# Where the top-k selection steps stand in the dilated branch's merge

## What is computed

```
proj = h @ w_in                                  # h = rmsnorm(x)
ya = forgetting_attention(qa, ka, va, log_f) * silu(za)     # branch A
yb = dsa_attention(qb, k, v, q_idx, kidx, widx) * silu(zb)  # branch B: top-256 keys per query by an indexer score
yc = dilated_attention(qc, kc, vc) * silu(zc)               # branch C
merged = sigmoid(ga)*(ya @ w_a) + sigmoid(gb)*(yb @ w_b) + sigmoid(gc)*(yc @ w_c)
out = rmsnorm(x + merged @ w_o)
```

## Time and profile before

| | us |
|---|---|
| median of 3 runs | 1481.98 |
| profiled execution, own time | 1478.63 |
| its span | 1476.6 |
| PE busy | 1416.3 (96%) |
| DVE busy | 715.2 (48%) |
| ACT busy | 686.4 (46%) |
| POOL busy | 72.0 (5%) |
| PE busy in the merge of branch C, 457 to 679 | 215.98 of 222 |

### The profile page before, as it was taken

How to read it: one execution, slowest core, us unless ns; L and a number is a source line. 1 busy time by engine, 2 the same in 40 slices (tenths; PEclk the granted TensorE clock), 3 DMA queues, 4 the chain that set the end, 5 groups by cost and what they waited for, 6 DMA issues and landing times.

```text
span 1476.6 us, 21005 instructions
## 1 busy us (share of the span) xinstructions
PE 1416.3 (96%) x7910; PEld 1121.4 (76%) x7910; DVE 715.2 (48%) x1618; ACT 686.4 (46%) x1510; POOL 72.0 (5%) x138
## 2 busy tenths in 40 slices
PE   5998899999999999999999989999999999999998
PEld 4976677777767777887777777777777778888786
DVE  4548655555656965463433444533343345222633
ACT  5457776667764531113555565454443533212312
POOL 3033100000000000000000000000000000000000
PEclk8999999999999999999999999999999999999999
DMA  6046111111111112222101001312223222232422
GB/s 207 22 116 156 50 37 29 36 30 36 37 36 29 44 43 79 78 72 72 30 22 29 23 15 52 106 37 72 72 72 101 58 86 51 64 81 70 167 89 100
DMA packets 107875, 96.26 MB, mean 65 GB/s; under 512 B 8320, under 2 KB 93696, under 8 KB 107520
## 3 DMA queue, kind: packets, MB, share of 16 engines
q1 hardware_dynamic: 96528, 58.21, 14.7%
q0 software_dynamic: 11248, 36.71, 7.9%
HBM read 72.62 MB, written 18.09 MB: 61 GB/s over the span
## 4 chain that ended last, share of the span: by engine, by line
PE 80%; DVE 5%; ACT 3%; issue 2%; DMA 0%; ACTq 0%; DVEq 0%; POOL 0%; POOLq 0%
PE bank L793 19%; PE bank L795 19%; PE bank L794 19%; PE bank L987 6%; PE bank L968 6%; PE slot L959 4%; PE slot L944 2%; DVE idle_out L1406 1%; PE slot L793 1%; PE slot L794 1%; PE slot L795 1%; ACT pta L1259 1%; ACT ptb L1259 1%; PE bank L913 1%; DVE tm L1663 0%
## 5 line engine op out<-in xcount | busy, mean ns | idle before, releaser
L793 PE MATMUL bank<-hs,w_hl 128*128 128x512 f32 x1088 | 436.4, 401 | 6.4 <-DVE tm L1663 5.5
L795 PE MATMUL bank<-hs,w_hl 128*128 128x512 f32 x1088 | 426.2, 392 | 0.0
L794 PE MATMUL bank<-hs,w_hl 128*128 128x512 f32 x1088 | 425.2, 391 | 0.0
L1379 DVE TENSOR_TENSOR w_hl<-w_raw,w_hl 128x512 fp32r<-128x512 f32 (+1 forms) x168 | 113.7, 678 | 342.7 <-ACT w_hl L1078 341.8
L793 PEld LDWEIGHTS bank<-hs,w_hl 128*128 128x128 f32 x1088 | 205.3, 189 | 48.6 <-issue 9.1
L795 PEld LDWEIGHTS bank<-hs,w_hl 128*128 128x128 f32 x1088 | 205.0, 188 | 44.6
L794 PEld LDWEIGHTS bank<-hs,w_hl 128*128 128x128 f32 x1088 | 205.6, 189 | 39.9
L1078 ACT ACTIVATE w_hl<-w_raw 128x512 fp32r<-128x512 f32 (+1 forms) x168 | 103.9, 621 | 171.0 <-PE bank L795 162.0
L1406 DVE TENSOR_SCALAR_CACHE_REDUCE idle_out<-score,state 128x768 uint8<-128x768 f32 (+3 forms) x140 | 115.4, 824 | 4.8
L1277 ACT ACTIVATE idle_out<-score,state 128x896 bf16<-128x896 f32 x64 | 70.3, 1098 | 17.1 <-DVE state L1402 16.0
L1576 DVE CUSTOM_DVE_ANT_0 slot<-slot,score 128x128 f32<-128x128 f32 (+7 forms) x64 | 47.3, 781 | 45.9 <-PE slot L959 45.9
(11 more groups left out here) (311 smaller groups left out, 2204.3 us busy)
## 6 DMA issues: line engine op xcount, KB each, us to landing
w_raw<-in_w_in_dram SPq DMA_DIRECT2D x136, 256.0 KB, 2.8
merged_scratch<-ms POOLq DMA_DIRECT2D x16, 512.0 KB, 3.6
ms<-merged_scratch POOLq DMA_DIRECT2D x16, 512.0 KB, 4.1
xn<-in_x_dram SPq DMA_DIRECT2D x8, 512.0 KB, 5.8
iq_st<-iq_hl POOLq DMA_DIRECT2D x32, 128.0 KB, 3.3
qb<-qb_scratch POOLq DMA_DIRECT2D x8, 512.0 KB, 5.0
w_raw<-in_w_o_dram SPq DMA_DIRECT2D x16, 256.0 KB, 3.7
qb_scratch<-bq_high POOLq DMA_DIRECT2D x4, 512.0 KB, 3.1
```

The lines of the kernel that those rows point to most:

```text
L793: pe.matmul(out_, wh, mh, start=start, stop=False)
L794: pe.matmul(out_, wh, ml, start=False, stop=False)
L795: return pe.matmul(out_, wl, mh, start=False, stop=stop)
L1379: v.tensor_tensor(lo, src, hi.bitcast(F32), ALU.subtract).then_inc(w_low, 1)
```

## The change

The counter that placed a step after every third piece goes. After each piece the code looks at the last block step in the list. A selection step is placed only if that piece was of half 0 and the tile is a gate tile `gc` (either base), or has base 0 and is an output tile `wc` or the gate-path tile `zc` 2 or 4. The loop that emptied the queue after the merge is replaced by an assertion that it is empty.

```
-    pieces = 0
     while fill:
         pump(1)
-        pieces += 1
-        if pieces % 3 == 0:
+        a = next(a for kind, a in reversed(plan) if kind == "block")
+        b = blocks[a["n"]]
+        if a["th"] == 0 and (b["kind"] == "gc" or b["base"] == 0 and (b["kind"] == "wc" or b["c"] in (2, 4))):
             pick()
     flush()
-    while picking:
-        pick()
+    assert not picking
```

## The result

The changed kernel takes 1472.45 us (median of 6 runs, 1470.39 to 1473.6), the kernel before in the same rounds 1480.78 (median of 6, 1478.51 to 1484.78). The ratio is 0.9939 with a 95% interval of 0.9927 to 0.995, so 8.3 us by the medians and 7.4 to 10.8 us by the interval. The forecast was 1475.2 us, with a range of 1471.8 to 1478.6, and a saving of 6.8.

The account below looks back on a forecast made before the run. PE was taken to set the end, idling only at bank waits in branch C's merge. Terms -7.0 + 0.2 = -6.8 us took the median 1481.98 to 1475.2 us, range 1471.8 to 1478.6.

Parts of the forecast that it names:

- four gaps: PE idles in the merge of branch C at zc2, after zc3, at zc5 and wc0; removing these saves 7.0 us.
- The dense bit steps: Bit steps 26 to 31, close together in gc0, gc1, wc0 and gc2; cost taken as 0.2 us.
- 13.45 worked out: In gc0, ACT's tanh of half 1 ends 13.45 us after the tile's first matmul; PE wants bank 1 at 13.65.
- margin of 0.25: After step 30 in wc0, DVE frees bank 0 at 29.8 us; PE wants it at about 30.0.
- margin of 0.2: At gc0 with step 27, ACT's tanh of half 1 ends 0.2 us before PE wants bank 1 again.
- stalls move into gc0 and gc1: Rival: steps 27 and 29 stall PE between gate halves; both give 1480.9 us (chance 0.04), only 27 gives 1477.8 (0.07).
- Steps 24 and 25: The two steps remaining in gate-path tiles zc2 and zc4, after the first piece; cost 0.
- the 18 DVE-only steps: One in each output tile and two in each gate tile, fitting the room DVE has there; cost 0.
- The end of the merge: The last step, three pieces later, still ends before the last tile is read; handover to the next stage as before.
- Banks as the cause: Rival: with one bank per half any order makes PE wait, so gaps only move; 1482.0 us, chance 0.03.
- the first part: The working on what bounds the kernel, which reads PE's timeline and finds that the merge loses 7.0 us.
- I keep this distance: The runs' median lies 3.35 us above the profiled execution; the same was assumed for the changed kernel, giving 1475.2 us.

Follow-up runs that it names:

- the fifth trace of the kernel before: The kernel before, unchanged, traced a fifth time: own time 1482.13 us, merge 227.37 us, clock 0.89 behind both large gaps.
- the first trace: The kernel before, unchanged, in the trace that the prediction used: own time 1478.63 us, merge 225.11 us, clock 1.00 behind both large gaps.
- the kernel with two steps back: Changed kernel with bit steps 24 and 25 put between the halves of zc2 and zc4: 1478.06 us, ratio 0.9984 to the kernel before.

## Why the prediction was right or wrong

- **PE sets the end, and the merge loses 7.0 us in four gaps: right.** The merge became 7.09 us shorter and is within 0.1 us of one without steps.
- **The dense bit steps: right in mechanism, and in one of the two narrow margins.** 13.44 us measured for 13.45 worked out. An added operation of 1.1 us came through by 0.9 us in front of gc2, as the margin of 0.25 says. At gc0 it came through whole, by 1.1: the margin of 0.2 was used up by the handover from ACT to PE, which is in no term of the sum. That nothing more was lost there owes something to luck. The 0.2 us that I took for this part was 0.1. The rival "stalls move into gc0 and gc1" did not come.
- **Steps 24 and 25, and the 18 DVE-only steps, at cost 0: right.** No gap stands near them.
- **The end of the merge: right.** The wait at the second broadcast is 1.20 us as before. (The last step moves five pieces later, from behind the 78th to behind the 83rd of 86, not three as the prediction says; it was still early enough.) Its danger was real: one step placed 2 pieces later costs 3.9 us.
- **Banks as the cause (what the Trainium skill's page "Perfetto Trace Analysis", section Optimization Strategy, says a repeating gap can mean): not so in this kernel.** With the same two banks all gaps are gone.
- **The size of the saving: wrong.** The step that failed is the one in the first part: "Less 0.23 each, that is 2.69 + 0.26 + 3.08 + 0.64 = 6.67 us", with a clock of 1.00. The term was put at -7.0 us, and it takes from one trace that a gap costs its own length. That trace was one of the three in five in which the clock did not fall behind the gaps. In the other two the merge is 2.3 us longer, so against them the change saves 9.4 us of the merge and not 7.1. Over all runs, 61 of the kernel before have a mean of 1480.8 us and 11 of the changed kernel one of 1471.8, 9.0 us apart. 7.1 of them are the gaps. The remaining 1.9 us fit a lower clock in the runs: the mean granted clock is on record for 55 of the 61, and it is 0.9917 there against 0.9942 in the 11. Among the 55 an execution is some 0.8 us longer for each 0.001 of clock, which makes 2.0 us (an estimate, from a straight line through the 55). That this clock was lost behind the gaps is shown in two traces and argued for the runs as a whole.
- **"I keep this distance"** of 3.35 us between the profiled execution and the median: wrong. For the changed kernel it is 0.25 us. 1.0 of it was the chance of three runs: their median was 1481.98, that of all 61 is 1480.95. The rest fits the lower clock above, since the one traced execution had its clock at 1.00 behind both gaps. So of the 2.7 us by which the forecast missed, 1.2 come from the time before (1481.98 taken, 1480.78 in the six runs) and 1.5 from the saving.

Open: two traces in five with 2.3 us more give a mean of 0.9, not 1.9. But the five traced executions are short ones (mean 1479.3 us, mean clock 0.9934, against 1480.8 and 0.9917), so on the whole they hold less of the low clock than the rest. Where in the untraced runs it fell is not on record, and the clock outside the merge differs between executions too: 15 us at 0.89 near 880 us are in both traces of the changed kernel and in two of five of before; with them the part behind the merge takes 798.4 us, without them 796.9. Among the changed kernel's eleven runs the time does not follow the clock (1470.76 us at 0.993, 1473.02 at 0.995). So how the 1.9 us divide was not settled.

## What to carry to other kernels

When a filler step is put into the queue of an engine that frees a bank, count what stands in front of the next bank read on that engine, and place the step where the read is farthest away. The kernel that moved two steps by one piece shows that "not between the halves" is no rule by itself. Do the same at the end of a stage. And a gap of 2 us or more on PE may cost more than its length: take several traces of the kernel before, and look for matmuls at double distance behind the gap.

## What the runs showed of the hardware

- In the kernel before, after the same wait of 2.5 us, PE ran at the 1.2 GHz level (matmuls 0.43 us apart in place of 0.23) in two executions and not in three. It fell behind both large gaps or behind none. In single traces of other kernels it fell after waits of 1.96, 2.4, 3.11 and 4.30 us. After waits of 0.90, 0.91 and 1.55 us in front of dense weight-tile matmuls it did not fall.
- The length of the wait alone does not say it: in the fifth trace of the kernel before the clock was also down from 441 us on (0.89 for 435 to 450), behind a longest wait of 1.11 us and among small matmuls with short waits between them, and the first trace has the same waits at this place without the fall.
- The time until it falls differs: in the fifth trace 0.3 to 0.6 us after PE's restart at the first gap and at once at the second, 1.3 us in the kernel with two steps back, at once at the first gap of the kernel with two steps moved.
- In the program with two equal gaps (a wait of 1.96 us each) the first was followed by such a stretch, the second not.
